# Stick-breaking keys and half of the queries computed feature-major with stationary weight blocks; linear attention's diagonal blocks one k tile later

## The reference

```
def stick_breaking_mixer(xn, w_qkv, w_o):          # 16 heads of 64
    q, k, v = split(xn @ w_qkv)
    z = einsum('qd,kd->qk', q, k) * 64 ** -0.5     # per head
    mask = key_pos < q_pos
    log_beta, log_1m_beta = log_sigmoid(z), where(mask, log_sigmoid(-z), 0)
    suffix = reverse_cumsum(log_1m_beta) - log_1m_beta
    weights = where(mask, exp(log_beta + suffix), 0)
    return (weights @ v) @ w_o                     # xn = x * rsqrt(mean(x^2)+eps) * gain
```

## Time and profile before

| | us |
|---|---|
| median of 3 runs | 1723.64 |
| lowest and highest run | 1723.12, 1724.19 |
| the profiled execution | 1722.8 |
| its span, first to last instruction | 1721.0 |

### The profile page before, as it was taken

One profiled execution on the slowest core, in us unless ns is written; L12 is line 12 of the kernel. 1 busy time (PEld: TensorE's weight loads), 2 busy tenths in 40 slices (PEclk: granted clock), 3 DMA queues, 4 the chain that ended last, 5 costly groups with the idle time before them and its releaser, 6 DMA issues. The chain is left out here.

```text
span 1721.0 us, 22917 instructions
## 1 busy us (share of the span) xinstructions
PE 1713.3 (100%) x8786; PEld 1431.1 (83%) x8786; DVE 1217.4 (71%) x1680; ACT 1045.3 (61%) x1623; POOL 167.1 (10%) x137
## 2 busy tenths in 40 slices
PE   9999999999999999999999999999999999999998
PEld 8888887788888878888888888888888888788887
DVE  7867667667777778766667766588776666786664
ACT  7665667757565766654565744477665446665542
POOL 0000011200000010211000210002021100102110
PEclk9999999999999999999999999999999999999999
DMA  9555453255555533555544555453455554336552
GB/s 366 202 196 185 174 204 141 86 190 220 185 186 186 190 124 122 210 193 196 189 187 165 217 187 186 166 208 147 159 208 196 187 181 183 133 112 222 187 192 72
DMA packets 45997, 311.62 MB, mean 181 GB/s; under 512 B 5472, under 2 KB 5856, under 8 KB 9664
## 3 DMA queue, kind: packets, MB, share of 16 engines
q1 hardware_dynamic: 45328, 309.00, 49.2%
q0 software_dynamic: 272, 1.05, 0.2%
q10 hardware_dynamic: 288, 0.11, 0.0%
HBM read 309.09 MB, written 1.05 MB: 180 GB/s over the span
## 5 line engine op out<-in xcount | busy, mean ns | idle before, releaser
L1397 DVE SCALAR_TENSOR_TENSOR wlo<-raw,first,whi 128x512 fp32r<-128x512 f32 x704 | 505.7, 777 | 108.5 <-ACT whi L746 108.0
L746 ACT ACTIVATE whi<-raw,first 128x512 fp32r<-128x512 f32 x704 | 452.8, 713 | 85.0 <-PE ps L2304 72.0
L2403 PE MATMUL ps<-xs,whi 128*128 128x512 f32 x1344 | 423.2, 396 | 0.0
L2302 PE MATMUL ps<-whi,xs 128*128 128x512 f32 (+1 forms) x896 | 358.6, 400 | 0.4 <-DVE wlo L1397 0.4
L2304 PE MATMUL ps<-whi,xs 128*128 128x512 f32 (+1 forms) x896 | 348.6, 389 | 0.0
L2303 PE MATMUL ps<-wlo,xs 128*128 128x512 f32 (+1 forms) x896 | 347.8, 388 | 0.0
L2406 PEld LDWEIGHTS ps<-xs,wlo 128*128 128x128 f32 x1344 | 252.4, 188 | 59.3
L2302 PE MATMUL ps<-whi,hhi 128*128 128x512 f32 x720 | 281.3, 391 | 0.0
L2303 PE MATMUL ps<-wlo,hhi 128*128 128x512 f32 x720 | 280.4, 389 | 0.0
L2304 PE MATMUL ps<-whi,hlo 128*128 128x512 f32 x720 | 280.2, 389 | 0.0
L1394 DVE TENSOR_TENSOR wlo<-raw,whi 128x2048 fp32r<-128x2048 f32 x110 | 250.8, 2305 | 26.9 <-ACT whi L737 26.9
(11 more groups left out here) (251 smaller groups left out, 1355.0 us busy)
## 6 DMA issues: line engine op xcount, KB each, us to landing
raw<-in_w_parts SPq DMA_DIRECT2D x283, 1024.0 KB, 4.8
gain<-in_gains SPq DMA_DIRECT2D x10, 512.0 KB, 6.4
raw<-in_w_parts SPq DMA_DIRECT2D x5, 512.0 KB, 8.5
x<-in_x SPq DMA_DIRECT2D x2, 512.0 KB, 10.5
arena<-in_bias_line POOLq DMA_DIRECT2D x1, 1024.0 KB, 13.1
out<-x SPq DMA_DIRECT2D x4, 256.0 KB, 2.0
proj<-in_x_turned SPq DMA_DIRECT2D x2, 256.0 KB, 4.0
raw<-in_w_parts SPq DMA_DIRECT2D x2, 256.0 KB, 4.0
```

The source lines that it names most:

```text
L746: nc.scalar.activation(whi[n % HIS][:, cols], raw[n % LOS][:, cols], ACT.Copy, scale=gcol[:, COLUMNS[n] + kk:COLUMNS[n] + kk + 1]).then_in ...
L1397: nc.vector.scalar_tensor_tensor(out=lo[:, cols], in0=whole[:, cols], scalar=gcol[:, COLUMNS[n] + kk:COLUMNS[n] + kk + 1], in1=hi[:, cols] ...
L2302: nc.tensor.matmul(out_ap, a_hi, wh, start=first, stop=False)
L2403: nc.tensor.matmul(ps[:, 4 + m, :], whi[n % HIS][:, kk * BANK + m * P:kk * BANK + (m + 1) * P], xs[:, k, :, :].rearrange("p h n -> p (h n) ...
```

## The change

In both stick-breaking stages the jobs j = 2, 3 and 4 (the first half of k and the second halves of q and k) are computed feature-major by `turned_job`. For each half jj of the k tiles and each pair u of weight blocks it takes four steps; the weaving function is called ahead of every step with (j, jj, 4u + kk). The transposes of b = 2 to 7 go, those of b = 0 and 1 stay and move. For each of the six tiles b = 2 to 7 ACT copies the lower half (`sb_lower`), DVE adds the upper half (`sb_sum`), and POOL multiplies by the row of norms (`scaled`). `rows_of_scales` is called once per stage, and ACT copies the row twice. PE gets new waits: for `tile_summed` ahead of the jobs 3, 4 and 5, for `tile_scaled` ahead of the scores. DVE's and ACT's orders are rewritten, the places of scores, sums and values in the PE queue are kept. In the linear-attention stage the diagonal blocks 0, 1 and 2 move from k = 3, 4, 5 to k = 4, 5, 6, and the state update stays at k = 5.

```diff
-QK_BANKS = {"mix_ab": 9, "mix_sb": 8, "mix_conv": 4, "mix_gla": 4}
+QK_BANKS = {"mix_ab": 9, "mix_sb": 2, "mix_conv": 4, "mix_gla": 4}
...
-            run["lin"] += 2 * s["doubles"]
+            run["lin"] += 3 if following["kind"] == "mix_sb" else 2 * s["doubles"]
+            run["rows"] += following["kind"] == "mix_sb"
...
+        ROW_Q = proj[:, 1, 4608 + SEQ:4608 + 2 * SEQ]
...
+        def split_banks(b, lower):
+
+            first = 4 if b % 2 == 0 else 0
+            return ps[:, first:first + 2, SEQ * lower:SEQ * (lower + 1)]
+
+        def tile_rows(b):
+
+            return turned_tiles(b).rearrange("p (m n) -> p m n", m=2)
...
+            def sb_lower(s, b):
+                act.wait_ge(job_done, s["n_job"] - 12 + nth_job(b // 2 + 1, b % 2))
+                nc.scalar.activation(tile_rows(b), split_banks(b, 1), ACT.Copy).then_inc(lower_ready, 1)
+
             def sb_lin(s, part0, evac):
 
+                act.wait_ge(row_ps, s["n_rows"])
+                nc.scalar.activation(ROW, ps[:, 3, 0:SEQ], ACT.Copy)
+                nc.scalar.activation(ROW_Q, ps[:, 3, 0:SEQ], ACT.Copy, scale=0.125).then_inc(row_ready, 1)
+                hi_to(part0 + 8, 2)
+                sb_copy(s, 0)
                 hi_to(part0 + 9)
-                evac(2, 0)
+                sb_lower(s, 2)
                 hi_to(part0 + 10)
-                sb_copy(s, 0)
-                evac(2, 1)
-                sb_copy(s, 2)
-                hi_to(part0 + 11)
-                evac(3, 0)
+                sb_lower(s, 3)
+                hi_to(part0 + 11, 2)
+                sb_lower(s, 4)
                 hi_to(part0 + 12)
-                evac(3, 1)
-                hi_to(part0 + 13)
-                sb_copy(s, 4)
+                sb_lower(s, 5)
                 sb_exp(s, 0)
                 sb_log(s, 0)
-                evac(4, 0)
-                hi_to(part0 + 14)
+                hi_to(part0 + 13)
+                sb_lower(s, 6)
                 sb_exp(s, 1)
                 sb_log(s, 1)
-                evac(4, 1)
+                sb_lower(s, 7)
                 sb_exp(s, 2)
                 sb_log(s, 2)
                 hi_to(part0 + 15)
-                sb_copy(s, 6)
                 sb_weights(s, 0)
                 sb_weights(s, 1)
...
+            def sb_sum(s, b):
+                dve.wait_ge(lower_ready, 6 * s["n_sb"] + b - 1)
+                nc.vector.tensor_tensor(tile_rows(b), split_banks(b, 0), tile_rows(b), ALU.add).then_inc(tile_summed, 1)
+
             def sb_lin(s, part0):
 
+                lo_to(part0 + 8, 2)
+                sb_copy(s, 1)
+                lo_to(part0 + 9)
+                sb_sum(s, 2)
                 lo_to(part0 + 10)
-                sb_copy(s, 1)
-                lo_to(part0 + 11)
+                sb_sum(s, 3)
+                lo_to(part0 + 11, 2)
                 sb_masked(s, 0)
                 sb_negated(s, 0)
-                sb_copy(s, 3)
+                sb_sum(s, 4)
+                lo_to(part0 + 12)
+                sb_sum(s, 5)
                 lo_to(part0 + 13)
+                sb_softplus(s, 0)
                 sb_masked(s, 1)
                 sb_negated(s, 1)
-                lo_to(part0 + 14)
+                sb_sum(s, 6)
+                sb_low(s, 0)
+                sb_masked(s, 2)
+                sb_negated(s, 2)
+                sb_sum(s, 7)
+                sb_softplus(s, 1)
 
             def mix_sb(s, part0):
...
-                sb_masked(s, 2)
-                sb_softplus(s, 0)
-                sb_softplus(s, 1)
-                sb_negated(s, 2)
-                sb_low(s, 0)
                 sb_masked(s, 3)
                 sb_low(s, 1)
+                lo_to(part0 + 2)
+                sb_softplus(s, 2)
                 sb_arg(s, 0)
-                sb_softplus(s, 2)
+                sb_low(s, 2)
                 sb_arg(s, 1)
-                sb_low(s, 2)
-                sb_copy(s, 5)
                 sb_negated(s, 3)
                 sb_arg(s, 2)
                 sb_masked(s, 4)
...
-                for p in range(8):
+                pool.wait_ge(row_ready, s["n_rows"])
+
+                def scaled(b):
+                    pool.wait_ge(tile_summed, 6 * s["n_sb"] + b - 1)
+                    row = ROW_Q if b in (4, 5) else ROW
+                    nc.gpsimd.tensor_tensor(tile_rows(b), tile_rows(b), row.unsqueeze(1).to_broadcast([P, 2, SEQ]), ALU.mult
+                                            ).then_inc(tile_scaled, 1)
+
+                def rounded(p):
                     pool.wait_ge(n_ready, p0 + p + 1)
                     if p >= 2:
                         pool.wait_ge(sum_done, p0 + p - 1)
                     nc.gpsimd.tensor_copy(SN_HI[p % 2], SA[p % 3]).then_inc(nhi_ready, 1)
+
+                for b in range(2, 6):
+                    scaled(b)
+                rounded(0)
+                scaled(6)
+                rounded(1)
+                scaled(7)
+                for p in range(2, 8):
+                    rounded(p)
...
+                def turned_job(j):
+
+                    for jj, n in enumerate(parts_of(j)):
+                        for u in range(2):
+                            if jj == 0 and j > 2:
+                                pe.wait_ge(tile_summed, 6 * s["n_sb"] + 2 * (j - 3) + u + 1)
+                            elif jj == 0 and u == 0:
+                                pe.wait_ge(lin_evac, base + 1)
+                            for kk in range(PANELS):
+                                k = PANELS * jj + kk
+                                between(mix, j, jj, PANELS * u + kk)
+                                if u == 0:
+                                    weights(n, kk)
+                                for m in range(2):
+                                    at = kk * BANK + (2 * u + m) * P
+                                    nc.tensor.matmul(ps[:, (4, 0)[u] + m, :], whi[n % HIS][:, at:at + P],
+                                                     xs[:, k, :, :].rearrange("p h n -> p (h n)"), start=(k == 0), stop=False)
+                                for m in range(2):
+                                    at = kk * BANK + (2 * u + m) * P
+                                    ins = nc.tensor.matmul(ps[:, (4, 0)[u] + m, 0:SEQ], wlo[n % LOS][:, at:at + P],
+                                                           xhi[:, k, :], start=False, stop=(k == KT - 1))
+                            if jj == 1:
+                                ins.then_inc(job_done, 1)
+                            elif u == 1:
+                                ins.then_inc(w_used, 1)
+
                 first_jobs(s, lin_bank, parts_of)
-                for j in range(2, jobs):
+                if s["woven_kind"] == "mix_sb":
+                    rows_of_scales(s)
+                    for j in (2, 3, 4):
+                        turned_job(j)
+                for j in range(5 if s["woven_kind"] == "mix_sb" else 2, jobs):
                     for t in range(NT):
-                        if tight and j > 2:
+                        if s["woven_kind"] == "mix_sb":
+                            pe.wait_ge(tile_summed, 6 * s["n_sb"] + 5)
+                        elif tight and j > 2:
...
-                if p // 2 % 2 == 0:
-                    pe.wait_ge(qk_act, s["n_qka"] + 2 + p // 4 * 2)
-                else:
-                    pe.wait_ge(qk_dve, s["n_qkd"] + 2 + p // 4 * 2)
+                if p < 2:
+                    pe.wait_ge(qk_act, s["n_qka"] + 1)
+                elif p < 4:
+                    pe.wait_ge(qk_dve, s["n_qkd"] + 1)
+                pe.wait_ge(tile_scaled, 6 * s["n_sb"] + (p // 2 + 1 if p < 4 else p // 2 + 3))
...
-                if at == (2, 1, 5):
+                if at == (2, 0, 6):
                     sb_turn(s, 0)
                     sb_turn(s, 1)
-                elif at == (3, 0, 2):
-                    sb_turn(s, 2)
                 elif at == (3, 1, 2):
                     sb_scores(s, 0)
-                elif at == (4, 0, 2):
-                    sb_turn(s, 3)
-                    sb_turn(s, 4)
                 elif at == (4, 1, 4):
                     sb_scores(s, 1)
-                    sb_turn(s, 5)
                 elif at == (4, 1, 7):
                     sb_scores(s, 2)
                 elif at == (5, 0, 2):
                     sb_scores(s, 3)
-                elif at == (5, 0, 3):
-                    sb_turn(s, 6)
                 elif at == (5, 0, 5):
                     pe.wait_ge(suffix_ready, 1)
                     sb_sums(s, 0)
...
                     sb_scores(s, 4)
                 elif at == (5, 1, 1):
                     sb_sums(s, 2)
-                    pe.wait_ge(qk_act, s["n_qka"] + 4)
+                    pe.wait_ge(tile_summed, 6 * s["n_sb"] + 6)
...
                     sb_scores(s, 5)
-                elif at == (5, 1, 3):
-                    sb_turn(s, 7)
                 elif at == (5, 1, 6):
                     sb_sums(s, 3)
                     sb_scores(s, 6)
```

(44 more changed lines are left out.)

5 lines of the change are left out of this document (3 added, 2 removed).

## The result

| | us |
|---|---|
| before, median of 7 runs beside those of after | 1723.62 (1723.12 to 1724.19) |
| after, median of 7 runs | 1728.67 (1725.79 to 1730.19) |
| after / before | 1.0027, 95% interval 1.0017 to 1.0038 |
| profiled execution of after, its span | 1728.2, 1726.4 |

A forecast was written before the change was run, and what follows sets the result against it. PE, busy 1713.3 of 1721.0 us, was taken as the bound. PE's work -3.7, waits 2 x 2.2 and linear attention -0.3 sum to +0.4 us: forecast median 1724.0 us, range 1719.6 to 1726.0.

The forecast's parts named there:

- PE's own work: Stick-breaking stages: PE's queue changes by -2.69 + 0.78 + 0.22 - 0.16 = -1.85 us a stage.
- form and tails: Changed jobs on PE: slower feature-major groups cost +0.78 us a stage, shorter tails behind four insertions give -0.16.
- the transposes: Stick-breaking stages: taking out the transposes of b = 2 to 7 saves PE 2.69 us a stage, tails included.
- the row of norms: Stick-breaking stages: the transposes that build it add 0.22 us a stage on PE.
- The wait at sums 1: Stick-breaking stages: PE waits at `sb_sums(1)` for DVE's arg 0, 2.2 us a stage, bounds 1.5 and 2.4.
- PE -1.85 + wait: Each stick-breaking stage changes by PE's own -1.85 us plus the 2.2 us wait at sums 1.
- The tile sums for jobs 3 and 4 are ready 0.8 us or more before PE asks: Stick-breaking stages: PE does not wait for these sums; tile 3 is the closest.
- What is late next is nothing that PE waits for: Linear attention: after the diagonal blocks move one k tile later, no new PE wait follows.
- The step's own gain: Linear attention: PE's 0.25 us idle ahead of the first diagonal block goes, gaining 0.3 us.
- A: Rival: no wait at sums 1, so the whole -4.0 us is kept, 1719.6 us; chance 0.22.
- B: Rival: POOL's products go first both times, low 0 held too, waits of 4.1 us a stage, 1727.8 us; chance 0.12.

The follow-up runs named there:

- e6: e1 plus 100 extra waits on a long reached semaphore among TensorE's instructions before linear attention; 1721.33 us, ratio 0.9988.
- e1: The kernel after, with DVE's weight part 13 moved behind arg 1 and softplus 2 behind arg 0; 1722.46 us, ratio 0.9996.
- e4: The kernel after, with POOL's product 7 moved behind rounding 2; 1724.46 us, ratio 1.0009.
- e5: e6 with weight part 13 made early and tile sum 3 one weight panel ahead; 1719.99 us, ratio 0.9980.
- e8: The kernel after, with 100 extra waits on a long reached semaphore among TensorE's instructions before linear attention; 1726.96 us, ratio 1.0020.
- e7: The kernel before, with 47 extra waits on a semaphore set at the start, among TensorE's matmuls before linear attention; 1724.95 us, ratio 1.0007.

## Why the prediction was wrong, point by point

- **PE's own work, forecast -1.85 a stage: right in sum, by terms that err both ways.** After's stage 1 is +1.06 - 2.41 (sums 1) - 0.41 (tile sum: 0.31 ahead of the matmul that waits, and 0.10 more until the next one) = -1.76. e6 has no wait at sums 1; its stages, -0.81 and -0.87, less 0.41 at the tile sum and 0.61 at scores 5, are -1.83 and -1.89. Summed start to start over the second stage of e6 against before, matmuls by kind: form and tails are +0.34 (forecast 0.78 - 0.16 = 0.62); the transposes fall from 3.06 to 0.79 us, -2.27 (forecast -2.69, which had tails in it that are in the other sum here); the row of norms is +0.14 (forecast 0.22); the suffix sums are -0.10 (not forecast). Two small slips of the working change nothing: its own numbers give -3.0 and not -3.1 as the weaker bound for two stages, and four tails at 0.13 - 0.08 are -0.20 and not -0.16.
- **The wait at sums 1, forecast 2.2, bounds 1.5 and 2.4: right.** 2.41 us, by the mechanism, the places and the order named; e1 and e4 confirm both halves, part 13 (1.60 us with the product out of the way) and product 7 (0.81 us). It is 0.4 us of the miss for two stages, because 2.2 stood between two cases of which only one happens.
- **"PE -1.85 + wait" as the whole of a stage: this step failed.** The sum had a price for the time in which PE stands and none for the clock behind it. The clock fell to 1.2 GHz for 3.41 us behind three of the six waits of this length in the profiles, 1.5 us each time. All rows of before were read at full clock, because before has no wait of this length. With zero, one or two such stretches the parts of the kernel after give about 1726.8, 1728.3 and 1729.8 us (1723.6 - 3.5 + 4.8 + 0.8 + 1.1, then 1.5 each); the seven runs lie from 1725.8 to 1730.2.
- **"The tile sums for jobs 3 and 4 are ready 0.8 us or more before PE asks": this step failed too,** by 0.31 us a stage, or 0.41 with the slower start behind it. The layout took part 9's panels at 0.75 us each. In the second stage of the kernel after, DVE's four panels of part 9, and sum 3 behind them, are

```profile
1454.45 3.80 DVE L1415 SCALAR_TENSOR_TENSOR wlo<-raw,first,whi 128x512 fp32r<-128x512 f32 x4
1458.17 0.68 DVE L1947 TENSOR_TENSOR arena<-ps,arena 128x512 f32<-128x512 f32 x1
```

  3.80 us and not 2.7, since one of them took 1.80 while POOL's product 2 ran (1.70 us from 1454.67). No run moved that product, so that it is what held the panel is argued, not tested: every panel of 1.8 us in these stages starts within a product. The prediction had the port's rule in hand for low 1, and did not apply it to the panels. e5, with the sum one panel earlier, has no such wait.
- **"What is late next is nothing that PE waits for" in linear attention: this step failed as well, +1.38 instead of nothing.** The step's own gain is there: 0.25 us of idle time is gone, 0.32 us start to start (forecast 0.3), and the stage is 0.43 and 0.38 us shorter in e6 and e8, which have the edit and no late fetch. The 1.38 us came over the instruction fetch. No step of the prediction counted TensorE's instructions.
- **Rivals.** A (no wait) is refuted by the first row of the waits. e5, in which the part is moved, comes near its time (1719.6 forecast, 1719.99 measured), but that is partly luck: it is 3.3 us below the before beside it, where A had 4.0. B (POOL first both times) did not happen: low 0 took 0.95 us in both stages, and no wait of 4.1 us is seen. What was called slower by over 0.2% with a chance of 0.10 happened, for neither of B's reasons.

In sum the median's miss of 4.7 us is 1.4 (gates), 1.5 (one half-clock stretch), 0.8 (tile sums), 0.4 (wait) and 0.2 (PE's own gain). That is 4.3; the remaining 0.4 lies within what the opening varies by.

## What to carry to other kernels

A wait of 2 us on a busy TensorE cost 1.5 us more than itself in three cases of six here, so price it with the clock behind it, and a spread between runs that grows is a hint at it. When an operation on VectorE is laid out beside GpSimd work, apply the port's rule to every operation in the window and not only to the one under suspicion. A change that leaves a stage untouched can still slow it by shifting instruction fetches into its loads; when a stage far from the edit waits for a DMA, compare the landings of its shares and the instruction fetches before looking for a reason in the schedule.

## What the runs showed of the hardware that was not expected

- The granted clock halved for exactly 3.41 us right behind an idle time of PE of 1.9 or 2.2 us, in three of six such waits, and behind none of the two of 1.4 us at sums 1. It came 0.3, 1.0 and 1.4 us after PE had gone on working.
- With one instruction fetch of 16 KB among the loads, a single share of a 1 MB load landed 1.2 to 1.5 us behind the others (after, e1 and e7: 13.44, 13.35 and 13.20 us against 11.9 to 12.1 for the slowest of the rest; 0.85 us in e4), although the fetch's packet took 0.92 to 1.15 us. One share of the load issued next was late by 1.2 to 1.5 us too (0.8 in e4).
- 100 extra wait instructions on TensorE between matmuls of 0.23 us cost nothing: the projections ahead of linear attention have the same length to 0.01 us (e6 against e1, e8 against after).
